# Late state-space steps and the first gated head's queue reordered, quarters of two up units fetched early

## What is computed

```python
def _mixer_cd(x, w_in, ...):
    proj = x @ w_in
    gq, gk, gv, gr, ga, sz, sxbc, sdt = _split(proj, GLA_SPLITS + SSD_SPLITS)
    log_alpha = jax.nn.log_sigmoid(ga @ gla_w_alpha + gla_b_alpha) / GLA_TAU
    y_gla = _head_norm(_gla(q, k, v, _heads(log_alpha, GLA_H)), ...) * jax.nn.silu(gr)
    xbc = jax.nn.silu(_causal_conv(sxbc, ssd_conv_w, ssd_conv_b))
    dt = jax.nn.softplus(sdt + ssd_dt_bias)
    y = _ssd(xs * dt, dt * a, bm, cm)                      # 16 heads in 4 groups
    y = (y + ssd_d * xs) * jax.nn.silu(sz)
    y_ssd = _head_norm(y, SSD_GROUPS, ssd_norm_g, False)
    return jnp.concatenate([y_gla, y_ssd], axis=-1) @ w_out
...
def _moe(x, w_router, b_router, w_gate, w_up, w_down):
    ...
    for e in range(N_EXPERTS):
        h = jax.nn.silu(xt @ w_gate[e]) * (xt @ w_up[e])
        y = y + combine[:, e:e + 1] * (h @ w_down[e])
```

## Time and profile before

| | us |
|---|---|
| median of 3 runs | 970.33 |
| lowest, highest | 970.25, 971.67 |
| the profiled execution | 971.41 |
| its span, first to last instruction | 969.6 |
| TensorE matmuls busy | 932.4 (96%) |
| VectorE, ScalarE, GpSimd busy | 381.3, 235.6, 69.7 |

### The profile page before, as it was taken

One profiled execution on the slowest core, in us unless ns is written; L12 is line 12 of the kernel. 1 busy time (PEld: TensorE's weight loads), 2 busy tenths in 40 slices (PEclk: granted clock), 3 DMA queues, 4 the chain that ended last, 5 costly groups with the idle time before them and its releaser, 6 DMA issues. The chain is left out here.

```text
span 969.6 us, 11314 instructions
## 1 busy us (share of the span) xinstructions
PE 932.4 (96%) x4464; PEld 569.7 (59%) x4464; DVE 381.3 (39%) x877; ACT 235.6 (24%) x514; POOL 69.7 (7%) x45
## 2 busy tenths in 40 slices
PE   8999999999999999999999999998999999999896
PEld 7888998744533453333587888895545334443332
DVE  4645585523522121120448746766125221121204
ACT  1123353420311120110303354524513111111101
POOL 2122122000000000000011201010000000000001
PEclk9999999999999999999999999998999999999999
DMA  8974434462999999999984253434447999999993
GB/s 272 344 264 171 148 125 162 159 233 107 346 385 421 421 421 421 405 420 416 391 323 162 88 217 119 185 131 174 174 173 268 374 422 422 419 421 418 419 417 147
DMA packets 66937, 278.92 MB, mean 288 GB/s; under 512 B 8980, under 2 KB 9344, under 8 KB 44096
## 3 DMA queue, kind: packets, MB, share of 16 engines
q1 hardware_dynamic: 65008, 271.60, 71.8%
q0 software_dynamic: 1872, 6.53, 1.8%
HBM read 277.04 MB, written 1.06 MB: 287 GB/s over the span
## 5 line engine op out<-in xcount | busy, mean ns | idle before, releaser
L792 PE MATMUL bank<-ring,feat 128*64 128x512 f32 (+1 forms) x1152 | 228.6, 595 | 3.0 <-ACT feat L1709 2.7
L792 PEld LDWEIGHTS bank<-ring,feat 128*64 128x64 f32 (+1 forms) x1152 | 73.8, 131 | 142.9 <-issue 131.3
L1709 ACT ACTIVATE feat<-bank 32x512 f32<-32x512 f32 (+3 forms) x128 | 60.9, 494 | 382.6 <-PE bank L792 242.6
L792 PE MATMUL bank<-ring,yT 128*128 128x512 f32 x256 | 114.4, 602 | 0.0
L792 PE MATMUL bank<-hT,ring 128*128 128x256 f32 x512 | 112.3, 380 | 1.0 <-DMA ring<-in_w_in_ab 1.0
L792 PE MATMUL bank<-ring,hT 128*64 128x512 f32 x416 | 101.5, 594 | 8.5 <-issue 4.8
L792 PEld LDWEIGHTS bank<-hT,ring 128*128 128x128 f32 x512 | 97.6, 192 | 14.1 <-DMA ring<-in_w_in_ab 1.7
L2691 DVE COPY feat<-bank 32x512 f32<-32x512 f32 (+1 forms) x56 | 38.5, 687 | 145.9 <-PE bank L792 145.3
L792 PEld LDWEIGHTS bank<-ring,yT 128*128 128x128 f32 x256 | 48.4, 193 | 56.4 <-issue 56.2
L2681 DVE TENSOR_TENSOR feat<-feat,bank 128x512 f32<-128x512 f32 x16 | 11.0, 688 | 170.0 <-PE bank L792 170.0
L792 PEld LDWEIGHTS bank<-ring,hT 128*64 128x64 f32 x416 | 36.3, 137 | 63.3 <-issue 59.2
(11 more groups left out here) (289 smaller groups left out, 991.1 us busy)
## 6 DMA issues: line engine op xcount, KB each, us to landing
ring<-in_moe_w_up SPq DMA_DIRECT2D x60, 1024.0 KB, 15.9
ring<-in_moe_w_down SPq DMA_DIRECT2D x56, 1024.0 KB, 11.8
ring<-in_moe_w_gate SPq DMA_DIRECT2D x48, 1024.0 KB, 14.3
ring<-in_w_in_ab SPq DMA_DIRECT2D x24, 1024.0 KB, 8.8
ring<-in_w_in_cd SPq DMA_DIRECT2D x24, 1024.0 KB, 13.4
ring<-in_w_out_ab SPq DMA_DIRECT2D x8, 1024.0 KB, 6.1
ring<-in_moe_w_gate SPq DMA_DIRECT2D x16, 512.0 KB, 5.2
ring<-in_moe_w_down SPq DMA_DIRECT2D x16, 512.0 KB, 17.1
```

Source lines behind the costliest of these rows:

```text
L792: return nc.tensor.matmul(o, l, r, start=start, stop=stop)
L1709: return nc.scalar.activation(o, i, f, **kw)
```

## The change

Four edits, all of order or place; nothing that is computed changes.

- VectorE, end of the state-space part: the arguments and products of groups 2 and 3 come ahead of the gates of groups 0 and 1, and the third blend of cd11 stands between the two products. The arguments of a group wait for the values of the group whose buffer they take. ScalarE: the exponentials of groups 2 and 3 come ahead of the last copy and the z unit of cd11 and of the squares of groups 0 and 1.
- VectorE, first gated head: the mix of cd3 moves into the loop of scans, behind scan 1; the third blend of cd2 moves ahead of the wait for the edges; the time-step columns take its place as head 0's `meanwhile`.
- The last two of eight rows (0.5 MB) of the first pair's second up unit go into feat instead of the ring, issued behind the first early half (layer 1) or behind the wait after it (layer 0), with a semaphore of their own.
- The same rows of the fourth pair's second up unit go into a free row of tok, issued behind the first early half, and are counted by `early_in`, which then has seven DMAs a layer.

```diff
--- before.py
+++ after.py
@@ -228,6 +228,9 @@
         early = ((as_unit(yT[:, 0:8, :]), as_unit(yT[:, 8:16, :])), (as_unit(tok[:, 0, :, :]), as_unit(tok[:, 3, :, :])),
                  (spare[:, :].rearrange("p (k n) -> p k n", n=FF), as_unit(tok[:, 2, :, :])))
         EARLY = len(early)
+        early_rows = tok[:, 1, 1, :].rearrange("p (k n) -> p k n", n=FF)
+        EARLY_IN = 16 * (2 * EARLY + 1)
+        first_rows = flat(feat[:, 18:22, :]).rearrange("p (k n) -> p k n", n=FF)
         lnp = tok[:, 2, :, :]
 
 
@@ -241,6 +244,7 @@
         down_used = sem("down_used")
         last_in = [sem(f"last_in{k}") for k in range(FF // P)]
         early_in = sem("early_in")
+        first_rows_in = sem("first_rows_in")
         out_used = sem("out_used")
         par_in = sem("par_in")
         par_late = sem("par_late")
@@ -620,8 +624,10 @@
 
                 def stream_two(n, k, src, half, es=range(2)):
 
-                    rows = slice(half * k // 2, (half + 1) * k // 2)
                     for e in es:
+                        rows = slice(half * k // 2, (half + 1) * k // 2)
+                        if half and n + e in (n0 + 3, n0 + 6 * EARLY_PAIR + EARLY):
+                            rows = slice(KC // 2, KC - 2)
                         sp.wait_ge(*freed(n + e - RING, half))
                         sp.dma_start(slot(n + e, k)[:, rows, :], src[e][:, rows, :]) \
                             .then_inc((ring_full, ring_rest)[half][(n + e) % RING], 16)
@@ -660,14 +666,22 @@
                     sp.dma_start(early[j][half], unit[:, half * (KC // 2):(half + 1) * (KC // 2), :]) \
                         .then_inc(early_in, 16)
 
+                def fetch_first_rows():
+
+                    sp.dma_start(first_rows, up[layer, 1][:, KC - 2:, :]).then_inc(first_rows_in, 16)
+
                 src_of_early = [pair[j][0][layer, 2 * EARLY_PAIR + pair[j][1]] for j in range(EARLY)]
                 y_last = ("y_ret3", "y_ssd3")[layer]
                 for half in range(2):
                     stream_two(n0, KC, gate[layer, 0:2], half)
                 sp.wait_ge(ready[first_of(y_last)], plan[y_last][first_of(y_last)] + 1)
                 fetch_early(1, 0)
+                if layer == 1:
+                    fetch_first_rows()
+                sp.dma_start(early_rows, up[layer, 2 * EARLY_PAIR + 1][:, KC - 2:, :]).then_inc(early_in, 16)
                 if layer == 0:
                     sp.wait_ge(ready[max(plan["yturn0_3"])], plan["yturn0_3"][max(plan["yturn0_3"])] + 1)
+                    fetch_first_rows()
                 else:
                     sp.wait_ge(sq_arg, KC)
                 fetch_early(1, 1)
@@ -1264,7 +1278,7 @@
 
                 def weights(pair, j, k):
                     if pair == EARLY_PAIR and j < EARLY:
-                        pe.wait_ge(early_in, 32 * EARLY * (layer + 1))
+                        pe.wait_ge(early_in, EARLY_IN * (layer + 1))
                         return lambda c: early[j][c // (KC // 2)][:, c % (KC // 2), :]
                     n = n0 + 6 * pair + j
                     if (pair, j) in ((1, 0), (1, 1)):
@@ -1275,6 +1289,11 @@
                     def part(c):
                         if c == k // 2:
                             rest_in(n)
+                        if (pair, j) == (0, 3) and c >= KC - 2:
+                            pe.wait_ge(first_rows_in, 16 * (layer + 1))
+                            return first_rows[:, c - (KC - 2), :]
+                        if (pair, j) == (EARLY_PAIR, EARLY) and c >= KC - 2:
+                            return early_rows[:, c - (KC - 2), :]
                         return unit[:, c, :]
 
                     return part
@@ -2089,12 +2108,12 @@
             sum_copy("cd10", 2)
             sum_copy("cd11", 0, 1)
             z_unit("cd10", 0)
+            ssd_exps(2)
+            ssd_exps(3)
             sum_copy("cd11", 2)
             z_unit("cd11", 4)
             squares(0)
             squares(1)
-            ssd_exps(2)
-            ssd_exps(3)
             norm_rows(0)
             norm_rows(1)
             squares(2)
@@ -2791,19 +2810,22 @@
                 link(V.tensor_tensor_scan(bcum[:, hd, :], dec[:, 0, 0:SEQ], gtmp[:, hd, :], 0.0, ALU.mult, ALU.add))
                 if hd == 1:
                     blend("cd2", 1)
-
-            mix_weights("cd3")
-            b0 = first_of("dt_cols")
-            wait_ready(dve, "dt_cols", b0)
-            link(V.tensor_copy(gate_col[:, 1, :, :], bank[b0][:, 0:32].rearrange("p (t n) -> p t n", t=TB)))
-            V.tensor_scalar(route[:, 5, :, :], bank[b0][:, 32:64].rearrange("p (t n) -> p t n", t=TB), -1.0,
-                            None, ALU.mult).then_inc(stored[b0], 1)
+                    mix_weights("cd3")
+
             refs = gate_col[:, 0, :, :].rearrange("p a b -> p (a b)").rearrange("p (h i) -> p h i", h=HEADS)
             step(V.tensor_scalar(edge[:, 0, :], bcum[:, :, P - 1], 1.0 / GLA_TAU, None, ALU.mult))
             step(V.tensor_scalar(edge[:, 1, :], bcum[:, :, P - 1], -1.0 / GLA_TAU, None, ALU.mult))
             V.tensor_scalar(refs, bcum[:, :, GLA_MID::GLA_BLOCK], 1.0 / GLA_TAU, None, ALU.mult) \
                 .then_inc(gate_a, 1)
+            blend("cd2", 2)
             dve.wait_ge(gate_a, 5)
+
+            def dt_columns():
+                b0 = first_of("dt_cols")
+                wait_ready(dve, "dt_cols", b0)
+                link(V.tensor_copy(gate_col[:, 1, :, :], bank[b0][:, 0:32].rearrange("p (t n) -> p t n", t=TB)))
+                V.tensor_scalar(route[:, 5, :, :], bank[b0][:, 32:64].rearrange("p (t n) -> p t n", t=TB), -1.0,
+                                None, ALU.mult).then_inc(stored[b0], 1)
 
             def gla_head(hd, meanwhile):
                 blocks = lambda x: x.rearrange("p (i c) -> p i c", c=GLA_BLOCK)
@@ -2853,7 +2875,7 @@
                     ins.then_inc(stored[b], 1) if t else step(ins)
 
             cw = ROWS_CD["conv_w"]
-            gla_head(0, lambda: blend("cd2", 2))
+            gla_head(0, dt_columns)
             blend("cd3", 0)
             mix_last("cd3")
             blend("cd3", 1)
@@ -2958,13 +2980,15 @@
             blend("cd11", 0)
             mix_last("cd11")
             blend("cd11", 1)
-            blend("cd11", 2)
-            ssd_gate(0)
+            wait_ready(dve, "y_ssd0", first_of("y_ssd0"))
             ssd_args(2)
-            ssd_gate(1)
+            wait_ready(dve, "y_ssd1", first_of("y_ssd1"))
             ssd_args(3)
             ssd_probs(2)
+            blend("cd11", 2)
             ssd_probs(3)
+            ssd_gate(0)
+            ssd_gate(1)
             ssd_gate(2)
             ssd_gate(3)
             for g in range(GROUPS):
```

## The result

| | before | changed |
|---|---|---|
| median, us | 970.25 | 963.74 |
| lowest to highest of 5 runs | 968.42 to 971.67 | 961.5 to 964.43 |
| profiled execution, its span | 971.41, 969.6 | 962.69, 960.9 |

The ratio is 0.9934, with a 95% interval of 0.9918 to 0.995: 6.5 us less, between 4.8 and 8.0. The kernel is faster, and its time lies in the range given.

A forecast was written before the change was run, and what follows sets the result against it. TensorE was taken as the bound, with the DMA queue bounding expert stages after its gap. Terms 6.3 + 0.3 + 1.4 = 8.0 us, off the 970.33 median, gave 962.3 us, range 959.2 to 965.4.

The forecast's parts named there:

- The reading of the bound: Whole kernel: TensorE is the engine to follow; expert stages are TensorE-bound up to the queue's gap, queue-bound after it.
- TensorE's three waits: Expert weights, 4.5 us in six; a VectorE product in the state-space stage, 3.3; a VectorE sum in first gated head, 1.3.
- the gap in the queue: Expert stages, after 392.0 and 880.5 us: DMA share falls to 0.49 and 0.81, as TensorE had not freed a slot.
- Part 1: Late state-space steps: reordering removes a 3.3 us TensorE wait and the low clock behind it, gaining 6.3 us.
- the clock's: State-space tail: 1.2 GHz level after the wait costs 1.3 us at group 2's values and 1.7 in the next projection block.
- Part 2: First gated head: earlier weight mix and third sum gain 0.3 us if GpSimd holds the scans, 1.4 if not.
- rival C: First gated head: scans and GpSimd don't meet, gain 1.4 us in place of 0.3, time 961.2 us; chance 0.15.
- Part 3: Expert stages: the first pair's quarter gains 0; the fourth pair's removes down-unit stalls of 0.46 and 0.97, gaining 1.4 us.
- Rival B: Expert stages: bandwidth bounds throughout, four quarters pay 1.25 us each, 5.0 in place of 1.4, 958.7 us; chance 0.11.
- A: State-space tail: a short wait remains and the low clock stays; 3.0 of 6.3 us stay, time 965.3 us; chance 0.12.
- E: State-space tail: new order takes no effect, as values of groups 0 and 1 release arguments later; 968.6 us; chance 0.03.
- D: State-space gates slip: free for 2.5 us, then one for one plus clock; slower beyond 7.5, 972.8 us at 10; chance 0.04.

The follow-up runs named there:

- seventh: Kernel before with only the seventh pair's second up unit's quarter (0.5 MB per layer) fetched early: 967.09 us, ratio 0.998.
- part3_first: Kernel before with only the first pair's quarter fetched early: 969.38 us, ratio 1.0004.
- gla_clear: Kernel before with the first gated head's cd3 mix behind scans and small reads, then cd2's third blend, and ScalarE's copies before head 0: 968.52 us, ratio 0.9983.
- part1_ssd: Kernel before with only the late state-space steps reordered on VectorE and ScalarE: 965.51 us, ratio 0.9962.
- cut_before_gap: Kernel before with 0.75 MB per layer of the fourth pair's second up unit not loaded, ahead of the queue's gap: 967.49 us, ratio 0.998.
- parts12: Kernel before with the late state-space and first gated head reorders, no quarter moved: 963.91 us, ratio 0.9942.
- whole_again: The changed kernel measured a second time, against the kernel before: 963.14 us, ratio 0.9939.
- cut_after_gap: Kernel before with 0.75 MB per layer of the seventh pair's second up unit not loaded, behind the queue's gap: 965.71 us, ratio 0.9969.
- slip12: Changed kernel with twelve chained idle-work VectorE instructions (7.09 us) ahead of the first gate: 969.93 us, ratio 1.0009 against the kernel before.

## Why the prediction was right, and where not

**The reading of the bound** held, with one omission. TensorE's three waits were the right places, and the gap in the queue is real. But "up to that gap its length is TensorE's with the stalls inside it" is too clean. The third pair of layer 0 and layer 1 shows it: 64 matmuls of one group took 13.90 and 14.22 us in before and 14.86 and 15.01 in the changed kernel:

```profile
307.83 14.86 PE L806 MATMUL bank<-ring,hT 128*64 128x512 f32 x64
...
787.38 15.01 PE L806 MATMUL bank<-ring,hT 128*64 128x512 f32 x64
```

The queue is late there. In the changed kernel a weight load in each of these two blocks waited for an up unit of the ring:

```profile
319.04 0.20 PEld L806 LDWEIGHTS bank<-ring,hT 128*64 128x64 f32 x4 [0.78 <-DMA ring<-in_moe_w_up]
...
798.74 0.20 PEld L806 LDWEIGHTS bank<-ring,hT 128*64 128x64 f32 x4 [0.93 <-DMA ring<-in_moe_w_up]
```

In before this wait was 0.2 us in layer 0 and absent in layer 1, and the stretch gets longer with it: in layer 1 `seventh` waited 1.0 us and lost 0.61, `part3_first` 0.3 and lost 0.09, and `gla_clear` has no such wait and gained 0.31. The first-pair quarter, an obvious suspect, is not the cause: `part1_ssd` and `cut_before_gap`, which have no early quarter, lose 0.89 and 0.85 us in layer 0, while `parts12` loses 0.05 and `whole_again` 0.55. It varies between executions and not with the edit. By 276 us `part1_ssd` and `cut_before_gap` had moved 59.46 and 59.44 MB, before 59.55 and `parts12` 59.58. The 0.1 MB less is 0.2 to 0.3 us at 420 GB/s, a part of their loss. What sets the rest stays open.

**Part 1.** Right in each step: arguments 2 done 2.72 us after their start, products by 663.6 (665.3 was forecast, and the whole kernel runs 1.6 us earlier here), gates last, margin 2.7 us (2.5 forecast), values 1.52, block 7.13 (7.0), clock 1.00. The 6.3 us stand in the trace to the hundredth, for both terms. The term mis-sized for the timed runs is the clock's, 3.0 us. The wait in front of it is 3.29 to 3.30 us in each kernel with the old order, but what follows is not fixed. `part3_first`, from its timeline:

```profile
672.91 2.83 PE L1650 MATMUL bank<-spare,tok 128*64 128x256 f32 x16 [3.30 <-DVE spare L2929]
675.67 7.16 PE L803 MATMUL bank<-ring,yT 128*128 128x512 f32 x16
```

The same place of `gla_clear`, and below it of `cut_before_gap`:

```profile
673.34 2.39 PE L1636 MATMUL bank<-spare,tok 128*64 128x256 f32 x16 [3.29 <-DVE spare L2918]
675.65 8.00 PE L792 MATMUL bank<-ring,yT 128*128 128x512 f32 x16
```

```profile
674.83 1.71 PE L1638 MATMUL bank<-spare,tok 128*64 128x256 f32 x16 [3.29 <-DVE spare L2917]
676.47 7.13 PE L794 MATMUL bank<-ring,yT 128*128 128x512 f32 x16
```

The first lost 1.4 us to the clock, the second 1.8. The third lost only 0.3, and not to the clock, which is nowhere low there. Windows of `part3_first`, and below them of `cut_before_gap`:

```profile
672.00:676.00 4.00, 3.09 (x17) 2.14 (x18) 3.77 (x9) 3.45 (x7) 1.09 (x2) 0.57 0.64 211
676.00:680.00 4.00, 4.00 (x10) 1.72 (x9) 1.41 (x4) 0.00 (x0) 0.00 (x0) 1.00 0.14 51
```

```profile
672.00:676.00 4.00, 1.17 (x12) 0.84 (x14) 3.97 (x12) 3.99 (x9) 1.09 (x2) 1.00 0.60 243
676.00:680.00 4.00, 4.00 (x16) 1.85 (x13) 3.00 (x8) 1.37 (x2) 0.00 (x0) 1.00 0.76 210
```

Before had 0.69 and 0.50 in these windows, and its low clock outlasted the idle by some 6 us; that of `part3_first` was over by 676, 3 us after TensorE had started again. By the column "clock SSD", where 2.94 is a place without any low clock, the seven profiled kernels with the old order show a price of 0.2, 1.3, 1.4, 1.5, 1.6, 1.7 and 1.8 us, and before's own profile 2.9, the highest of eight. The typical value is 1.5, so part 1 is typically worth 3.3 + 1.5 = 4.8 us and not 6.3. That lies inside the interval of `part1_ssd` (2.2 to 5.2 us) and of `parts12` (4.3 to 7.0). I had read one execution as if its clock were a constant.

**Part 2.** Right: the scans are held, 3.56 us together, which leaves TensorE a wait of 0.92, and 0.29 us come out for the 0.3 taken; the timed run of this part alone shows no gain (1.0009). The Trainium skill (SBUF — State Buffer, "Who interferes with whom") has the rule that an instruction of VectorE with two SBUF inputs contends with one of GpSimd that reads SBUF; that it holds for a scan is now in a trace of this case, and rival C, which gave scans a pass, falls. The two scans end 1.27 us after GpSimd, since scan 2 is held to its end and scan 3 follows.

**Part 3.** The first pair's quarter is worth 0 (1.0004), as said. The fourth pair's stall is gone in both layers, and its stretches are 0.64 and 1.17 us shorter where the stalls had 0.46 and 0.97. The 0.2 us more, the same in both, is not explained. It is not the other wait for a down unit that before's waits from 325 to 365 hold (us in total, times, longest), for in the changed kernel that one is still there:

```profile
PEld bank L792 <- DMA ring<-in_moe_w_down: 0.8, 2, 0.5
```

```profile
PEld bank L806 <- DMA ring<-in_moe_w_down: 0.3, 1, 0.3
```

The gap is wider in layer 0, as said, and 1.5 us (0.2 to 2.9) were measured for 1.4. Rival B, all quarters at 1.25 us, falls: two of four gave nothing. In layer 0 its place was behind the gap, where `seventh` and `cut_after_gap` find it.

**The sum.** Expected from before's profiled execution were 8.0 us; measured are 6.5 (4.8 to 8.0) and 5.9 by the second ratio. The profiled executions differ by 8.7 us of span, which looks like a hit but holds 1.5 us of the clock episode at the start, which has nothing to do with the change, and 1.4 us by which before's low clock cost more than the typical 1.5. Set right for the typical clock, the steps give 4.8 + 0.3 + 1.4 = 6.5. The parts measured alone sum to 3.7 − 0.9 − 0.4 + 1.5 = 3.9 us, less than the whole's 5.9, but each has an interval of ±1.4, so this sum can't be told from it, and no interplay between the parts is shown. The forecast of 962.3 is 1.4 under the median found. It was also taken from a median of three runs, 970.33. Taken from the 968.86 of 28 runs it would have been 960.9, and 963.1 was measured beside them, 2.3 us more: the end time looked better than the gain, since a high start and too large a gain offset each other. That closeness was luck; the mechanism was not.

**Rivals.** A and E fall to the trace (clock 1.00, no wait), B and C to the runs above. D was not what happened, but its price is confirmed by `slip12`.

## What to carry to other kernels

In this kernel an idle stretch of TensorE costs itself and a clock penalty that differs from one execution to the next (0 to 2.9 us here behind 3.3); count the wait fully, and give the penalty a range from several executions. When an order is changed, look for the margin at the resource that the moved work frees (here the bank), for up to it a delay is free and beyond it can be dearer than one for one (4.4 us cost 7.0 here). Before taking bytes out of a queue, find where the queue last ran dry: in layer 0, where it ran dry plainly, bytes ahead of that point paid only a stall and bytes behind it nearly their whole length; in layer 1 no such difference was seen. And where one engine's instruction holds another's, place it where the held one has nobody waiting.

## What the hardware showed that was not expected

- The same 3.3 us of idle TensorE, with the same work around it, was followed in seven of eight executions by a low clock that cost 1.3 to 2.9 us, and in one, `cut_before_gap`, by none.
- Shorter idle stretches of TensorE can be followed by it too: in the expert stages of `gla_clear` the clock is 0.82 from 420 to 424, behind 2.8 us of idle, and 0.73 from 904 to 908, behind 2.0; in `seventh` it stays 1.00 from 896 to 908 with 2.4 us of idle among them. In the table it costs nothing that can be seen ("queue L0" of `gla_clear` is −0.04, "queue L1" −0.02), which fits stretches that hang on the queue.
- In some executions the clock is below 1.00 between 56 and 64 us, though the trace has no wait of TensorE from 40 to 64. The changed kernel has it in `whole_again` and not in its first profile. The two windows in before, and in that first profile:

```profile
56.00:60.00 4.00, 4.00 (x20) 2.90 (x19) 1.56 (x2) 0.00 (x0) 0.00 (x0) 0.89 1.05 389
60.00:64.00 4.00, 4.00 (x14) 3.29 (x13) 0.00 (x0) 1.21 (x3) 0.00 (x0) 0.69 1.05 388
```

```profile
56.00:60.00 4.00, 4.00 (x22) 3.00 (x21) 1.56 (x2) 0.00 (x0) 0.00 (x0) 1.00 1.06 386
60.00:64.00 4.00, 4.00 (x20) 3.54 (x19) 0.00 (x0) 1.21 (x3) 0.00 (x0) 1.00 1.05 386
```

  It costs some 1.6 us, and only the timed runs average over it.
- A VectorE blend that takes one input from a bank keeps its 0.42 us under a running GpSimd instruction; a scan or a subtraction with both inputs in SBUF doesn't.
